# The v product of the expert layers turned round, and three of four convolution chunks computed as diagonal matrix products

## What is computed

```
y_a = conformer_conv(a_val, a_gate, conv_w, conv_b, ln_g, ln_b)
...
o = rms_norm(o, gla_norm_g).reshape(B, S, hv).astype(h.dtype)
y_b = o * jax.nn.silu(r)
return jnp.concatenate([y_a, y_b], axis=-1) @ w_out
```

```
act = jax.nn.gelu(jnp.einsum('td,ted->te', ht, u[et]), approximate=False)
return jnp.einsum('te,ted->td', gt * act, v[et])
```

## Time and profile before

| | |
|---|---|
| three timed runs | 2706.79, 2711.13, 2711.04 us; median 2711.04 |
| profiled execution | 2704.2 us, span 2702.4 us, mean granted clock 0.958 |
| PE busy | 2496.0 us (92%) |
| DVE, ACT, POOL busy | 1720.0 (64%), 1297.0 (48%), 466.0 us (17%) |
| both V loops | 379.4 and 368.8 us |
| even layer, from the last u to the last sum for xT | about 50 to 232.7 us |

### The profile page before, as it was taken

The page is one execution under the profiler, slowest core; times in us unless marked ns, Lnnn a source line. Parts: engine busy times, 40 slices in busy tenths (PEclk is TensorE's granted clock), DMA queues, the critical chain, the costliest instruction groups (busy, mean ns, idle before and its releaser), DMA issues.

```text
span 2702.4 us, 47390 instructions
## 1 busy us (share of the span) xinstructions
PE 2496.0 (92%) x19556; PEld 2407.8 (89%) x19556; DVE 1720.0 (64%) x3162; ACT 1297.0 (48%) x2447; POOL 466.0 (17%) x390
## 2 busy tenths in 40 slices
PE   7277999999999999888899999999999988997899
PEld 6267999999999999865799999999999977787899
DVE  3864699877777767534469987775555543534654
ACT  4124544576544444444444456654444443453543
POOL 4900000188500000000000018850000000001000
PEclk9668999999999999999899999999999988999999
DMA  6103355544477777530235554446556553223352
GB/s 239 50 32 125 102 182 185 164 133 129 138 265 250 252 240 251 225 125 32 94 125 183 185 172 131 128 141 196 185 182 185 182 212 134 85 94 122 128 187 79
DMA packets 93220, 422.17 MB, mean 156 GB/s; under 512 B 10296, under 2 KB 12880, under 8 KB 85072
## 3 DMA queue, kind: packets, MB, share of 16 engines
q1 hardware_dynamic: 93008, 419.16, 46.8%
HBM read 415.96 MB, written 3.16 MB: 155 GB/s over the span
## 4 chain that ended last, share of the span: by engine, by line
PE 88%; DVE 6%; ACT 4%; issue 1%; POOL 0%; DMA 0%; SPq 0%; DVEq 0%; POOLq 0%; ACTq 0%
PE PS L170 88%; ACT mem L181 2%; DVE mem L192 2%; ACT r_sh L181 1%; DVE mem L184 1%; DVE r_sl L184 1%; DVE hT L192 1%; PE PS L173 0%; DVE mem L204 0%; ACT L180 0%; DVE xT L184 0%; DVE mem L198 0%; ACT r_hhi L181 0%; POOL hT L184 0%; DVE hT L188 0%
## 5 line engine op out<-in xcount | busy, mean ns | idle before, releaser
L184 DVE TENSOR_TENSOR r_sl<-mem,r_sh 128x1024 fp32r<-128x1024 f32 (+3 forms) x742 | 891.8, 1203 | 756.0 <-ACT r_sh L181 753.1
L181 ACT ACTIVATE r_sh<-mem 128x1024 fp32r<-128x1024 f32 (+3 forms) x742 | 765.1, 1033 | 510.7 <-PE PS L170 469.4
L170 PE MATMUL PS<-r_hhi,r_sh 128*128 128x256 f32 x3280 | 840.3, 292 | 101.1 <-ACT r_sh L181 66.4
L170 PE MATMUL PS<-r_hlo,r_sh 128*128 128x256 f32 (+1 forms) x3152 | 790.7, 287 | 17.6 <-DVE r_hlo L184 15.8
L170 PEld LDWEIGHTS PS<-r_hhi,r_sh 128*128 128x128 f32 x3280 | 644.2, 196 | 110.2 <-issue 57.2
L170 PEld LDWEIGHTS PS<-r_hlo,r_sh 128*128 128x128 f32 (+1 forms) x3152 | 616.5, 196 | 20.2 <-DVE r_hlo L184 17.6
L170 PE MATMUL PS<-r_ch,r_sh 128*128 128x256 f32 x2048 | 504.1, 283 | 0.0
L170 PE MATMUL PS<-r_cl,r_sh 128*128 128x256 f32 x2048 | 503.2, 283 | 0.7 <-DVE r_cl L184 0.7
L170 PE MATMUL PS<-r_hhi,r_sl 128*128 128x256 f32 x3280 | 469.9, 286 | 2.0 <-DVE r_sl L184 2.0
L181 ACT ACTIVATE mem<-PS 128x256 f32<-128x256 f32 (+22 forms) x629 | 215.2, 351 | 512.1 <-PE PS L170 485.9
L189 POOL TENSOR_SCALAR xT<-cst,mem 128x128 f32<-128x128 f32 x256 | 327.5, 1291 | 621.9 <-ACT mem L181 558.1
(11 more groups left out here) (126 smaller groups left out, 2238.2 us busy)
## 6 DMA issues: line engine op xcount, KB each, us to landing
mem<-in_u SPq DMA_DIRECT2D x256, 512.0 KB, 3.6
mem<-in_v SPq DMA_DIRECT2D x256, 512.0 KB, 4.3
mem<-in_w SPq DMA_DIRECT2D x16, 2048.0 KB, 8.2
mem<-in_ada SPq DMA_DIRECT2D x48, 512.0 KB, 4.1
mem<-in_in SPq DMA_DIRECT2D x9, 2048.0 KB, 8.4
mem<-in_wq SPq DMA_DIRECT2D x8, 2048.0 KB, 8.5
mem<-in_od_in SPq DMA_DIRECT2D x6, 2048.0 KB, 9.2
mem<-in_ev_in SPq DMA_DIRECT2D x5, 2048.0 KB, 10.6
```

What stands on the lines that cost most here:

```text
L170: return self.did(self.e and self.e.matmul(out, lhsT, rhs, start=start, stop=stop, skip_group_check=skip))
L181: return self.did(self.e and self.e.activation(out, in_, func, **kw))
L184: return self.did(self.e and self.e.tensor_tensor(out, a, b, op))
```

## The change

There are two parts. In the V loop the operands are exchanged: the coefficients (128 experts x 128 tokens, t = 0, 1) are the stationary operand, and 512 channels of the piece (q = 0, 1) stream past. An iteration is 12 matmuls of 512 columns, which fill the banks 4 to 7 as [token, channel]. After the loop ACT and DVE copy two banks each into `mixed`, PE turns them with 16 transposes of 128x128 into banks 0 to 7, and DVE adds these to `xT`. In the even layer c = 0, 1, 2 of the convolution go to PE: for each tap a diagonal matrix of its 128 weights is the stationary operand and `up` shifted by w the moving one, in plain float32, 31 matmuls of 256 columns per c. DVE builds the diagonals, up to four per operation (24 operations), in a ring of six slots. POOL keeps c = 3 alone. The products of r, the GLA's output, the mean and the norm change places in the order of PE, ACT and DVE, and the seven levels take three pairs of banks in the order 0, 6, 5, 4, 3, 2, 1.

```diff
+    DIAG = [(c, w) for c in range(3) for w in range(0, 31, 4)]
+    diag = [chunks((yTf if i < 4 else of)[:, 512 * (i % 4):512 * (i % 4) + 512], 4) for i in range(6)]
+    LEVELS = (0, 6, 5, 4, 3, 2, 1)
...
         for w in range(1, 31):
...
+            po.wait_ge(*po.tensor_tensor(taps[:, w % 2, :], up[:, 3, w:w + 256], cw, MUL).then_inc("tapP"))
+            po.tensor_tensor(y[:, 3, :], y[:, 3, :], taps[:, w % 2, :], ADD).then_inc("convP", w)
...
-            if lv % 2:
-                n = {5: 17, 3: 18, 1: 19}[lv]
-                hi(ac, n + 1)
-                evict(n)
...
+        def convolved(c):
+            ac.wait_ge("tapped", c, 28)
+            ac.activation(y[:, c, :], PS[:, c % 2, 0:256], ACT.Identity, bias=P("cb", c)).then_inc("convA", c)
...
+        def diagonals(*which):
+            for i in which:
+                c, w = DIAG[i]
...
+                if i >= 6:
+                    ve.wait_ge("tapped", *DIAG[i - 6])
+                ve.tensor_tensor(diag[i % 6][:, 0:n, :], ident.rearrange("p (o e) -> p o e", o=1).broadcast_to([128, n, 128]),
+                                 taps_c, MUL).then_inc("diag", i)
         for n in range(17):
             lo(ve, n + 1)
             evict(n)
-        conv(8)
+            if n >= 11:
+                diagonals(n - 11)
+        lo(ve, 18)
...
-            conv(2)
...
+        diagonals(6)
...
+            if lv == 6:
+                diagonals(7)
...
-        conv(31)
+            if i < 6:
+                diagonals(8 + i)
+        diagonals(*range(14, 22))
...
+        def convolve(c):
+            bank_wait(pe, c % 2)
+            for i, (at, w0_) in enumerate(DIAG):
+                if at != c:
+                    continue
+                pe.wait_ge("diag", i)
+                pe.wait_ge("u", c)
+                for w in range(w0_, min(w0_ + 4, 31)):
+                    last = pe.matmul(PS[:, c % 2, 0:256], diag[i % 6][:, w - w0_, :], up[:, c, w:w + 256], w == 0, w == 30)
+                last.then_inc("tapped", c, w0_)
+            emptied[c % 2] = ("convA", c)
...
+                def product(q, t, c, v, start=False, stop=False):
+                    return pe.matmul(PS[:, 4 + 2 * q + t, :], c[:, 128 * t:128 * t + 128], v[:, 512 * q:512 * q + 512], start, stop)
...
+                if j < 127:
+                    for q, t in banks:
+                        product(q, t, ch, h, start=j == 0)
+                    pe.wait_ge("c_lo", layer, j)
+                    for q, t in banks:
+                        product(q, t, cl, h)
                     pe.wait_ge("lo", V[j])
-                    for c in range(8):
-                        m = pe.matmul(OUTS[c], l[:, c, :], ch, False, False, skip=True)
+                    for q, t in banks:
+                        m = product(q, t, ch, l)
                     m.then_inc("wdone", V[j])
...
+                for t in range(2):
+                    last = pe.transpose(PS[:, c, 128 * t:128 * t + 128], mixed[:, 2 * q + t, 128 * (c % 4):128 * (c % 4) + 128], ident)
+                last.then_inc("turned", layer, c)
+                emptied[c] = ("x", k, c)
```

More of the change, by code:

```diff
@@ L664, in even_ac @@
             i = ac.activation(yT[:, c, :], y[:, c, :], ACT.Silu, scale=P("lng", c), bias=P("lnb", c))
-        ac.wait_ge(*i.then_inc("actC"))
+        i.then_inc("actC")
+        evict(20)
+        ac.wait_ge("out", 20)
         ac.activation(hhi[:, 0:1024], yTf[:, 0:1024], COPY).then_inc("yhi", 0)
[L667 to L672, removed]
-            hi(ac, n)
[L674 to L681, removed]
+        hi(ac, EV_OUT[1])
+        ac.activation(rTf, rTf, ACT.Silu).then_inc("silu_r", 0)
+        for n in EV_OUT[2:5]:
+            hi(ac, n)
         ac.wait_ge("yb", 0)
         ac.activation(hhi[:, 1024:2048], yTf[:, 1024:2048], COPY).then_inc("yhi", 1)
-        for n in EV_OUT[4:]:
+        for n in EV_OUT[5:]:
             hi(ac, n)
@@ L740, in even_ve @@
         ve.tensor_tensor(kd, kf, w2, MUL).then_inc("kd", 0)
-        conv(3)
         ve.wait_ge("zero", "A")
-        for lv in range(7):
+        for i, lv in enumerate(LEVELS):
             ve.wait_ge("lmm", lv)
@@ L801, in even_pe @@
         block_R(pe, EV_IN[13:17], (5, 6), ("out", 16))
[L802 to L804 removed]
+        def convolve(c):
[9 more added lines that the diff above has]
+            emptied[c % 2] = ("convA", c)
+        convolve(0)
+        for i, lv in enumerate(LEVELS):
             q_, k_ = (qf, kf) if lv == 0 else (qlb[lv - 1], klb[lv - 1])
@@ L866, in even_pe, with gate_r @@
             emptied[b] = ("o", par)
+        bank_wait(pe, 3)
+        pe.wait_ge("convP", 30)
+        pe.wait_ge("convA", 2)
+        for c in range(4):
+            last = pe.matmul(PS[:, 3, 0:256], ones, y[:, c, :], c == 0, c == 3)
+        last.then_inc("mean", 0)
+        emptied[3] = ("meanS", 0)
+        def gate_r(n):
+            block_T(pe, n, R_BANK[n - 17], ("out", n))
+        gate_r(17)
+        gate_r(18)
+        pe.wait_ge("osq", 0)
+        for i in range(2):
+            bank_wait(pe, 4 + i)
+            last = pe.matmul(PS[:, 4 + i, :], ones, o2[:, 512 * i:512 * i + 512], True, True)
+            emptied[4 + i] = ("oln", i)
+        last.then_inc("oss", 0)
+        bank_wait(pe, 2)
+        pe.wait_ge("ysq", 0)
+        for c in range(4):
+            last = pe.matmul(PS[:, 2, 0:256], ones, y2[:, 256 * c:256 * c + 256], c == 0, c == 3)
+        last.then_inc("var", 0)
+        emptied[2] = ("varL", 0)
+        gate_r(19)
+        gate_r(20)
         def out(n):
@@ L876, in out @@
             emptied[c] = ("x", 0, c)
-        for n in range(3):
-            out(n)
-        pe.wait_ge("osq", 0)
-        for i in range(2):
-            bank_wait(pe, 4 + i)
-            last = pe.matmul(PS[:, 4 + i, :], ones, o2[:, 512 * i:512 * i + 512], True, True)
-            emptied[4 + i] = ("oln", i)
-        last.then_inc("oss", 0)
-        for n in range(3, 16):
+        for n in range(16):
             out(n)
@@ L1061, in peer_ac @@
                     hi(ac, V[j + 1])
+            for i in (0, 2):
+                ac.wait_ge("mixed", layer, i)
+                ac.activation(mixed[:, i, :], PS[:, 4 + i, :], COPY).then_inc("rows_a", layer, i)
         def hots_ac(ac, g):
@@ L1327, in peer_pe @@
                     m.then_inc("wdone", V[j])
-                modulation_pe(pe, j)
-            for i in range(4):
-                emptied[4 + i] = ("x", k, 2 * i + 1)
+                else:
+                    pe.wait_ge("c_lo", layer, j)
+                    pe.wait_ge("lo", V[j])
+                    for q, t in banks:
+                        product(q, t, ch, h)
+                        product(q, t, cl, h)
+                        product(q, t, ch, l, stop=True).then_inc("mixed", layer, 2 * q + t)
```

149 lines of the change are left out of this document (77 added, 72 removed).

## The result

The changed kernel takes 2649.03 us (median of four runs, 2647.78 to 2655.14) against 2711.09 of the kernel before (four runs, 2706.79 to 2711.84): ratio 0.9788, 95% interval 0.9776 to 0.9799, so 62.1 us less. The profiled execution took 2649.24 us.

A forecast was written before the change was run, and what follows sets the result against it. PE's matmuls were taken to bound the V loops, DVE's convolution the even layer's start. V loops 33.5 - 5.4 = 28.1 us plus even layer 32.6 gave 60.7 us less: 2650 us, own range 2638 to 2663.

The forecast's parts named there:

- PE's sum: Even layer behind the levels: PE's products follow one another, first output matmul at 175.6 us instead of 194.35.
- the beat: V loops: 2.75 us per iteration instead of 2.88; forecast wrong if outside 2.72 to 2.78.
- one gap over 0.5 us between 118 and 171: Even layer: forecast wrong if PE has gaps over 0.5 us between 118 and 171 us.
- V loops, per iteration: V loops: 12 matmuls at 0.229 us replace 24 at 0.120, 0.132 us less per iteration, 33.5 us for 254.
- Rival 1: V loops: a wide matmul costs little beyond its columns, 0.216 us each, total 2611 us; chance 0.10.
- rival 2: V loops: cost goes by the column, 0.240 us per wide matmul, no gain in the loop, total 2684 us; chance 0.07.
- V loops, end: After the last iteration: copies and transposes ahead of the sums cost 2.7 us more per loop, 5.4 us for both.
- Rival 4: Layer 0's V loop: tiles come too late, it keeps its beat, 16.8 us lost, total 2667 us; chance 0.06.
- Even layer, to the merges: Even layer's convolution: POOL ends at 98 to 102 us, seventh set of diagonals at 101.2, merges start at 108.3.
- The second step that failed: Ahead of the merges: PE's taps end at 107.2 us and the first level's products, ending last, at 108.3.
- rival 3: Even layer: PE stays at half the clock in c = 1 and half of c = 2, costing 20 us, total 2671; chance 0.13.
- the full clock from 112 us on: Even layer: PE was to run at full clock from 112 to 171 us.

The follow-up runs named there:

- the pair of kernels without the norms' two orders: DVE instead of POOL computes the low parts of chunks 3 and 7 in each norm: 2638.27 us in the changed kernel, 2698.45 us in the kernel before.
- The kernel without the taps: The changed kernel with taps 1 to 30 of the convolution's last quarter (c = 3) left out on POOL, that part left uncomputed: 2633.06 us.
- the one with the pause: The changed kernel, where POOL waits ahead of tap 17 until the levels' last merge and computes taps 17 to 30 behind it: 2638.21 us.

## Why the prediction was right, and where it was wrong

The total was right: 60.7 us forecast for the sum, 60.4 in the stages, 60.2 in the pair of kernels without the norms' two orders. That it came so near is luck: two terms were wrong in opposite directions, the V loops' by 7.4 and the even layer's by 7.7 us. The mechanism held in the V loops and in PE's sum behind the levels; up to the merges it didn't. Of the signs that I had set, the beat (2.72) lies just on the edge of its range, and PE has one gap over 0.5 us between 118 and 171, 0.80 us at 141 for ACT's copy of the keys; it lay inside the 3.6 us taken for keys and state.

**V loops, per iteration: right in mechanism, the term too small.** "I take 0.229, between them": it is 0.2267, next to the shorter burst's 0.2275 of the earlier trace rows. So 40.6 us for 254 iterations instead of 33.5. The longer burst's 0.231 was no steady distance. Rival 1 (0.216) and rival 2 (0.240) both fall: the cost isn't by column, and it isn't small, it is 13.3 ns per matmul. At 256 and 512 columns alike the distance of this kernel's fp32r matmuls in the V loop is the columns' time and 13.3 ns; the Trainium skill's isolated gap ("TensorE: Matmul & The Clock Gate", Back-to-back issue gap), N/2.4 + 2.5 ns, has 215.8 for 512, and the trace doesn't agree.

**V loops, end: right.** 6.5 us after the last iteration's start forecast, 6.3 measured. Rival 4 (tiles late in layer 0) gave back little: the stage gained 17.1 us where layer 1 gained 18.4. One delay of 0.33 us at 733 us ends with ACT's copy of a piece.

**Even layer, to the merges: the step that failed.** "POOL [...] will end at 98 to 102 us": it ended at 109.2. I had scaled its operations by 0.55, from a 256-column operation of a norm (0.78) to the 512-column mean beside DVE (1.41). POOL's rows in the change, and its last tap's add:

```profile
L184 POOL TENSOR_TENSOR mem<-mem 128x256 f32<-128x256 f32 x30 | 27.8, 928 | 2.4
L184 POOL TENSOR_TENSOR mem<-mem,col 128x256 f32<-128x256 f32 x30 | 25.6, 852 | 2.4
...
108.37 0.79 POOL L184 TENSOR_TENSOR mem<-mem 128x256 f32<-128x256 f32 x1
```

The add's mean was 0.93 us, 0.66 of 1.41, and the multiply's 0.85; with short waits that is 1.9 us a tap from 51 to 109. So the last differences, for which I had taken 0.39 each near 100 us, took 0.8, and the twelve products 0.59 on average. The softplus stood at 87.01 (87.5 forecast), but the seventh set was done at 102.84 instead of 101.2. The second step that failed is what ends last: I had PE's taps and first level there, at 108.3. PE had these at about 109.8, and DVE's row of products held the merges until 112.25. The kernel without the taps shows the cause, and the one with the pause that it is POOL's place and not its amount. The Trainium skill ("SBUF — State Buffer", two separate sides) says that a blocked engine waits out the other's whole instruction; the trace agrees, with 0.82 us for each difference beside POOL and 0.36 without it.

**PE's sum: right but for the clock.** Merges and sets took 15.6 us (15.4 forecast), c = 2 13.65 (13.4), GLA 6.0 (5.6), keys and state 2.4 (3.6). But PE left the levels 11.8 us after the first merge instead of 9.9, and c = 1 took 15.8 instead of 13.4 (its window from 124 to 140 us, above, has a mean of 0.86). PE was granted half the clock there, though busy without a gap (PE's busy time is the third number, 13.00 of 13.00 us, and the clock is 0.50):

```profile
115.00:128.00 13.00, 13.00 (x67) 11.76 (x65) 12.47 (x30) 0.00 (x0) 0.00 (x0) 0.50 0.00 0
```

That is 4.3 us, rival 3's mechanism at a fifth of its 20 us. The first output stands at 182.57 instead of 175.6, and the next norm at 207.84 where I had the last sum at 200.1: 7.7 us late. 4.0 of them were there at the merges, 4.3 are the clock's, and keys and state gave 1.2 back; the rest is under 1 us in all.

**What I hadn't priced: the norms.** In the profiled executions the stretches behind two of them take 5.2 of the 5.4 us by which the spans' 55.0 fall short of 60.4: the late order 2.8 and 2.4, while the 1.6 us of half clock cancel, since each kernel has them once. That the late order costs this is shown by the edit of the norms: the stages behind the change's three late norms get 2.4, 2.7 and 4.4 us shorter (in the last, 1.6 are the stretch of half clock, which that trace doesn't have). What decides between the orders stays open. At the norm ahead of the first expert layer all five traces that have the change's even layer, with POOL's taps at their place and POOL's low parts, are in the late order; the two with the even layer of before are not. The one with POOL's pause has the late order too, the one without the taps doesn't. Yet the kernel before gained 10.4 us in its median from the edit and only 5.2 in its profiled span (2702.4 to 2697.2). That would fit if its timed executions were often in the late order where its profiled one wasn't, but no trace of such an execution exists, so it isn't shown.

## What to carry to other kernels

Read a matmul's cost as columns plus a constant from two rows of different width, and turn operands so that the stream is as wide as a bank allows; here that was worth 40 us, and what it cost was 2.5 us of transposes per loop. When work leaves one engine, ask at what time the engine that keeps the rest will be done, and whether the rest can lie where nobody waits: moving 14 taps of POOL by 30 us gave 11. Work of PE that fits into its waits keeps its clock as well: the two blocks of r between the levels gave 4.8 us, 1.4 of them by the clock. And a pair of engines that block each other should not share a handshake on the critical path.

## Not expected of the hardware

- POOL's r_hlo took 4.08 us beside a gapless row of DVE operations and 0.76 when they took turns. The 4.08 us were the same to a hundredth of a us each time. In the norms where POOL computes shifted chunks, every trace with r_hlo on POOL has them where POOL's first TENSOR_SCALAR had taken 0.92 us, and not where it had taken 2.00; which of them is cause is not shown. In the late order the two engines don't take turns: POOL's one operation lasts through DVE's whole row.
- 256-column fp32r matmuls stood 120.0 ns apart whether or not the stationary operand was new; 512-column ones 226.7.
- I had forecast the full clock from 112 us on. Behind the gap of 9.02 us PE was granted half the clock, and the full one from 108 to 114 us. Behind the wait of 1.46 us, during which the full clock still stood, it fell to half again for 115 to 128 us, in which PE had no gap. The window that holds the change:

```profile
112.00:124.00 12.00, 10.54 (x70) 9.94 (x68) 11.53 (x27) 0.00 (x0) 0.00 (x0) 0.61 0.00 0
```
